# Gate rows of the second block through a scratch row in device memory, and a regrouped opening

## The reference

```python
h = h + 0.5 * rmsnorm(swiglu(rmsnorm(h, g[0]), ffn1_w_in[i], ffn1_w_out[i]), g[1])
...
h = h + rmsnorm(mix, g[3])
h = h + 0.5 * rmsnorm(swiglu(rmsnorm(h, g[4]), ffn2_w_in[i], ffn2_w_out[i]), g[5])
h = h + rmsnorm(sigmoid(h @ ple_w_gate[i]) * (p[i] @ ple_w_proj[i]), g[6])
```

```python
sh1, sc1, g1, sh2, sc2, g2 = jnp.split(s_lat @ ada_w[i] + ada_b[i], 6, axis=-1)
a_l = modulate(rms_norm(h_lat, norm_g[i, 0]), sh1, sc1)
...
h_lat = h_lat + g1 * y_l            # one gate value per column, the same for all tokens
h_lat = h_lat + g2 * sq_relu_mlp(modulate(rms_norm(h_lat, norm_g[i, 1]), sh2, sc2), w1, w2)
```

## Time and profile before

| | |
|---|---|
| median of 3 runs | 1859.18 us (1859.07 to 1860.43) |
| the profiled execution | 1859.91 us, span 1857.8 us |
| PE busy | 1839.6 us, 99% |
| DVE, ACT, POOL busy | 1370.5, 950.6, 127.7 us |
| DMA | 380.68 MB, mean 205 GB/s |

### The profile page before, as it was taken

The page is one execution under the profiler, slowest core; times in us unless marked ns, Lnnn a source line. Parts: engine busy times, 40 slices in busy tenths (PEclk is TensorE's granted clock), DMA queues, the critical chain, the costliest instruction groups (busy, mean ns, idle before and its releaser), DMA issues.

```text
span 1857.8 us, 23263 instructions
## 1 busy us (share of the span) xinstructions
PE 1839.6 (99%) x9008; PEld 1522.6 (82%) x9008; DVE 1370.5 (74%) x1649; ACT 950.6 (51%) x1414; POOL 127.7 (7%) x177
## 2 busy tenths in 40 slices
PE   9999999999999999999999999999999999999998
PEld 6788888888878887887888888888888888888886
DVE  7898866977879777845598987777676558766665
ACT  5444564544464445544465435754564447555443
POOL 0430001000010000000020001100200001000000
PEclk9999999999999999999999999999999999999999
DMA  9787434877568775554496865545555546226552
GB/s 346 270 294 260 165 141 129 288 255 265 201 207 291 238 261 192 183 186 158 140 324 224 292 205 192 177 143 203 184 181 182 192 171 204 92 91 215 182 182 91
DMA packets 197374, 380.68 MB, mean 205 GB/s; under 512 B 13616, under 2 KB 101424, under 8 KB 197264
## 3 DMA queue, kind: packets, MB, share of 16 engines
q1 hardware_dynamic: 194336, 370.88, 58.5%
q0 software_dynamic: 2208, 7.73, 1.2%
q10 hardware_dynamic: 720, 0.58, 0.1%
HBM read 378.11 MB, written 1.05 MB: 204 GB/s over the span
## 4 chain that ended last, share of the span: by engine, by line
PE 93%; DVE 4%; DMA 1%; ACT 1%; issue 1%; POOL 0%; ACTq 0%; DVEq 0%; POOLq 0%; SPq 0%
PE ps L514 16%; PE ps L515 16%; PE ps L519 16%; PE ps L507 8%; PE ps L509 8%; PE ps L508 8%; PE ps L1312 7%; PE ps L531 4%; PE ps L1317 4%; DVE w_lo L2355 1%; DMA raw<-ffn_w_in_dram 1%; PE ps L762 1%; PE ps L1460 1%; PE ps L720 1%; PE ps L1484 1%
## 5 line engine op out<-in xcount | busy, mean ns | idle before, releaser
L2355 DVE TENSOR_TENSOR w_lo<-raw,w_hi 128x1024 fp32r<-128x1024 f32 x600 | 713.0, 1226 | 147.8 <-ACT w_hi L1612 143.4
L1612 ACT ACTIVATE w_hi<-raw 128x1024 fp32r<-128x1024 f32 x599 | 610.6, 1055 | 231.5 <-PE ps L519 139.8
L514 PE MATMUL ps<-w_hi,xt 128*128 128x512 f32 x692 | 275.5, 398 | 0.0
L515 PE MATMUL ps<-w_hi,xt 128*128 128x512 f32 x692 | 269.9, 390 | 0.0
L514 PE MATMUL ps<-w_hi,ht_hi 128*128 128x512 f32 x664 | 261.4, 394 | 0.2 <-DVE ht_lo L2560 0.2
L515 PE MATMUL ps<-w_hi,ht_lo 128*128 128x512 f32 x664 | 258.5, 389 | 0.0
L507 PE MATMUL ps<-w_hi,xt 128*128 128x512 f32 (+1 forms) x588 | 231.2, 393 | 3.9 <-DVE xt L2626 1.9
L509 PE MATMUL ps<-w_hi,xt 128*128 128x512 f32 (+1 forms) x588 | 227.6, 387 | 0.0
L508 PE MATMUL ps<-w_lo,xt 128*128 128x512 f32 (+1 forms) x588 | 227.3, 387 | 0.0
L2539 DVE SCALAR_TENSOR_TENSOR tmp<-arena,s_col,tmp 128x1024 f32<-128x1024 f32 x168 | 210.2, 1292 | 0.0
L519 PE MATMUL ps<-w_lo,xt 128*128 128x512 f32 x692 | 185.0, 389 | 0.0
(11 more groups left out here) (309 smaller groups left out, 2024.8 us busy)
## 6 DMA issues: line engine op xcount, KB each, us to landing
raw<-mlp_w_dram SPq DMA_DIRECT2D x192, 512.0 KB, 4.4
raw<-ffn_w_in_dram SPq DMA_DIRECT2D x168, 512.0 KB, 5.7
arena<-ada_w_dram SPq DMA_DIRECT2D x96, 512.0 KB, 6.2
raw<-ffn_w_out_dram SPq DMA_DIRECT2D x88, 512.0 KB, 4.5
raw<-odd_w_in_dram SPq DMA_DIRECT2D x48, 512.0 KB, 4.7
raw<-attn_w_qkv_dram SPq DMA_DIRECT2D x24, 512.0 KB, 4.9
raw<-even_w_in_dram SPq DMA_DIRECT2D x22, 512.0 KB, 4.6
raw<-ple_w_gate_dram SPq DMA_DIRECT2D x16, 512.0 KB, 3.9
```

Source lines behind the costliest of these rows:

```text
L514: pe.matmul(dst, a_hi, hi, start=start, stop=False)
L515: pe.matmul(dst, a_lo, hi, start=False, stop=False)
L1612: act.activation(w_hi[:, slot, c], raw[:, slot, c], ACT.Copy).then_inc(S(f"hi{slot}"), 1)
L2355: TT(w_lo[:, slot, c], raw[:, slot, c], w_hi[:, slot, c].bitcast(F32), ALU.subtract).then_inc(S(f"lo{slot}"), 1)
```

## The change

Gate rows: `gate_row`, `gate_copy` and the waits for them go. After each layer's conditioning vectors are done, ACT writes the gate columns to a tensor `gate_rows` in device memory, with one DMA for each gate (`gates_out(0)` four, `gates_out(1)` two, each of 128 x 8 single elements of 4 bytes), and later reads each row back with a DMA that broadcasts 4 KB to 128 partitions (`gate_in`, seven). `gates_out(0)` stands on ACT where the first half-row copy stood in `ffn(3)`.

```diff
+            def gates_out(l):
+                act.wait_ge(S("mod_set"), l + 1)
+                for j, part in enumerate((2, 5)):
+                    for v in range(2 - l):
+                        act.dma_start(T["gate_rows"][l, j, v].rearrange("(k p) -> p k", p=P), ada_of(l, part, v),
+                                      allow_slow_non_contiguous=True).then_inc(S("gates_out"), 16)
+
+            def gate_in(dst, signal, l, part, v):
+                act.wait_ge(S("gates_out"), (64, 96)[l])
+                act.dma_start(dst[:], T["gate_rows"][l, part // 3, v].partition_broadcast(P)).then_inc(S(signal), 16)
...
                 if run == 3:
-                    act.wait_ge(S("mod_set"), 1)
-                    gate_copy(table, 0, 6)
+                    gates_out(0)
                 split((1,) if run == 0 else (0, 1))
...
+                    if run == 3 and i == 3:
+                        gate_in(table, "gate_c", 0, 2, 1)
...
-                if i == 0:
-                    gate_row(0, 5, 0, (0, 1), 6)
-                elif i == 1:
-                    gate_row(1, 2, 0, (0, 1), 6)
-                elif i == 7:
+                if i == 7:
                     wait_xn()
                     xn_fill(0, xn_c)
...
                     act.wait_ge(S("p_free"), 8)
-                    gate_copy(gain, 0, 6)
-                    gate_copy(gain, 1, 7)
+                    gate_in(gain, "gate_l", 0, 5, 0)
+                    gates_out(1)
```

Opening: the host lays input and first weights side by side (`first_t`, 3 KB per partition and k) and SP alone loads them, one DMA per k (k = 3 in two). ACT issues only `norm_t`. The highs and lows are made as before, from `first_w` in `arena`. PE begins a k with its two products of highs and waits for each low only ahead of the products that read it:

```diff
+                    pe.wait_ge(S("x_hi"), 2 * k + 2)
+                    for m in range(MT):
+                        pe.matmul(bank(m), xt_hi[:, k, m * P:(m + 1) * P], hi, start=k == 0, stop=False)
                     if k in (0, 2):
                         pe.wait_ge(S("lo_first"), k // 2 + 1)
-                    elif k != 5:
+                    else:
                         slab(slot, uses, k // 2 % 2)
+                    for m in range(MT):
+                        pe.matmul(bank(m), xt_hi[:, k, m * P:(m + 1) * P], lo, start=False, stop=False)
                     pe.wait_ge(S("x_lo"), 2 * k + 2)
                     for m in range(MT):
-                        last = products(k, m)
+                        last = pe.matmul(bank(m), xt_lo[:, k, m * P:(m + 1) * P], hi, start=False, stop=False)
```

Small rows: `attn_sinks` and `hgrn_onorm_g` are laid in one array `mix_rows` by the host and loaded with one broadcast of 136 floats:

```diff
-                        first_rows()
+                        sp.dma_start(small[:, 120:256], T["mix_rows"].partition_broadcast(P)).then_inc(S("rows_in"), 16)
```

More of the change, by code:

```diff
@@ L282, in build @@
         rd = small[:, 80:96]
[L283 removed]
+        sink_b = small[:, 120:128]
         onorm_b = small[:, 128:256]
@@ L404, in ffn @@
                     sp.dma_start(vec_t[:], T["vec_cols"]).then_inc(S("vec_in"), 16)
-                    load(wide(wo, 0))
+                    slot, uses = ring.take()
+                    sp.wait_ge(S(f"hi{slot}"), 2)
+                    for src, view in wide(wo, 0):
+                        sp.dma_start(view(slot), src).then_inc(S(f"raw{slot}"), 16)
                     ada_load(run, 0)
@@ L736, in wait_xn @@
                 pe.wait_ge(S("xn_dve"), n["xn"])
[L738 to L745, removed]
             def pool_turn(src, g, b):
@@ L1756, in ffn @@
                 k = (n["sq"] - 1) % 4 if run else 0
-                split((0, 1), "raw2_half" if run == 0 else None)
+                split()
                 def swish(j, k_back, b0=4):
@@ L1849, in _ @@
             for half in range(2):
[L1850 to L1856, removed]
+                act.wait_ge(S(f"raw{s1}" if half else "raw1_half"), 32)
+                k = 4 + 2 * half
+                act.activation(cut(w_hi[:, s1, 1024 * half:1024 * half + 1024], 2, 512), first_w[:, k:k + 2],
+                               ACT.Copy).then_inc(S(f"hi{s1}"), 1)
+                first_high(k)
+                first_high(k + 1)
             n["x"] += 1
@@ L2585, in ffn @@
                     split()
-                    ada_sums(third)
-                    gated(base + i + 1)
+                    if run == 0 and i == 1:
+                        gated(base + i + 1)
+                        ada_sums(third)
+                    else:
+                        ada_sums(third)
+                        gated(base + i + 1)
                     if run == 0 and i == 5:
-                        dve.wait_ge(S("rows_in"), 64)
+                        dve.wait_ge(S("rows_in"), 32)
                         TT(lb_diff, lb_in[:, 0], lb_in[:, 1], ALU.subtract).then_inc(S("e_lb_in"), 1)
@@ L2634, in _ @@
                 c = slice(512 * k, 512 * k + 512)
-                TT(w_lo[:, s0, c], raw[:, s0, c], w_hi[:, s0, c].bitcast(F32),
+                TT(w_lo[:, s0, c], first_w[:, k], w_hi[:, s0, c].bitcast(F32),
                    ALU.subtract).then_inc(S(f"lo{s0}") if k % 2 else S("lo_first"), 1)
@@ L2638, in _ @@
             for half in range(2):
-                split_half(s1, u1, half)
-                first_low(4 + 2 * half)
-                first_low(5 + 2 * half)
+                dve.wait_ge(S(f"hi{s1}"), half + 1)
+                k, c = 4 + 2 * half, slice(1024 * half, 1024 * half + 1024)
+                TT(cut(w_lo[:, s1, c], 2, 512), first_w[:, k:k + 2], cut(w_hi[:, s1, c].bitcast(F32), 2, 512),
+                   ALU.subtract).then_inc(S(f"lo{s1}"), 1)
+                first_low(k)
+                first_low(k + 1)
             n["x"] += 1
@@ L2960, in gated_sums, with gated_add @@
                     TT(h[:, m, c], h[:, m, c], cut(tmp[:], 2, MT, 512)[:, half, m], ALU.add).then_inc(S(upd), 1)
-            def gated_add(m, h, gate, gates, upd, k_back):
-                dve.wait_ge(S("gate_set"), gates)
+            def gated_add(m, h, gate, landed, count, upd, k_back):
+                dve.wait_ge(S(landed), count)
                 if m == 0:
```

154 lines of the change are left out of this document (65 added, 89 removed).

## The result

The changed kernel takes 1876.16 us (median of five runs, 1866.11 to 1880.68) against 1859.18 before (1859.07 to 1860.43): ratio 1.0081, 95% interval 1.007 to 1.0091. It is slower, clear of the interval, and outside the forecast range. The runs of the kernel before lie within 1.4 us of each other, these within 15. The profiled execution is the fastest of the five: 1866.11 us, span 1864.0. So the trace shows 6 of the 17 us of the median; the other executions of this kernel have no trace.

A forecast was written before the change was run, and what follows sets the result against it. PE, busy 99% of the span, was taken to bound the kernel: 1859.9 - 4.4 (turns) - 1.5 (opening) - 0.9 (sinks) + 1.0 (writes) = 1854.1, as a median 1853.4 us. Range 1851.5 to 1860, likeliest case 1851.8 to 1855.4.

The forecast's parts named there:

- The opening: Start of kernel: x_t and first weights in order on SP bring the next stage to 18.0 us, saving 1.5 us.
- The sinks: Near 66 to 90 us: sinks and onorm as one broadcast end SP's hold and PE's wait, saving 0.9 us.
- The turns: Gate turns on PE: 48 fewer at two sites of four and five of eight, saving 4.4 us.
- the last site: Last site of eight turns: saves nothing, since PE sits idle 1.58 us behind it until DVE has xt ready.
- The broadcasts: Seven gate-row reads on ACT, 512 KB each: cost 0, covered by PE's products; uncovered, 4.2 us at a reader.
- The writes: Element writes ahead of the splits near 946 us: ACT held 2.8 us, PE stalled about 1.0 us.
- the positions end: Rate bound from the positions load, some 500 packets per us: 2 us for a write of 1024 elements.
- 2T - 3.4: Stall near 946 us in terms of T, the time of one 1024-element write; gains gone at T = 5.1.
- Rival 1: Slow element writes hold ACT, 946 to 965 us: stall 12 us at the sinks rate, total 1864.4; chance 0.13.
- Rival 2: The writes starve SP's weights as well: 31 us without weights, 22 us lost, total 1874; chance 0.05.
- The slack: Splits near 946 us: without a hold, a slip of 1.2 against a slack of 3.4 costs 0.

The follow-up runs named there:

- opening: Kernel before with only the change's opening and small rows, gates still by turns and copies: 1857.55 us, ratio 0.9989.
- blocks_late: Kernel of 512-byte gate pieces (blocks) with the four write issues moved from ahead of run 3's splits to the end of step 1: 1854.34 us, ratio 0.9971.
- spread: Changed kernel with the four writes of gates_out(0) issued on ACT one per step, in steps 0 to 3 of ffn(3): 1863.77 us, ratio 1.0019.
- pool: Changed kernel with the same element writes issued from POOL instead of ACT: 1868.43 us, ratio 1.0045.
- pair: The run writes with two of its four element writes ahead of run 3's splits: 1872.07 us, ratio 1.0067.
- none: The run writes without its four element writes ahead of run 3's splits, the two later ones kept: 1857.54 us, ratio 0.999.
- blocks: Changed kernel with each gate turned once on PE, copied once per layer and written as eight pieces of 512 bytes: 1855.66 us, ratio 0.9977.
- writes: The run opening, turns and copies kept, plus the six element writes into a scratch row nobody reads: 1873.36 us, ratio 1.0076.
- spaced: The run writes with each 4-byte element placed 512 bytes from the next: 1864.5 us, ratio 1.0027.
- gates: Kernel before with the gate part of the change alone, on the old opening: 1871.31 us, ratio 1.006.
- run 7: Not a run's label: in "its fastest run 7" the 7 is the loss in us of the changed kernel's fastest run, 1866.11 us.

## Why the prediction was wrong

- **The opening: right, and by the forecast road.** Forecast 1.5 us and 18.0 for the first product of the next stage; 18.04 measured. Between 5 and 6 us the DMA engines move 379 GB/s instead of 278. The last lows on DVE are done at 15.08 instead of 16.16, and the last twelve products begin right behind them (timelines of DVE and PE):

```profile
14.20 0.88 DVE L2605 SCALAR_TENSOR_TENSOR xt<-arena,norm_t,xt 128x256 fp32r<-128x256 f32 x2
```

```profile
15.22 0.47 PE L505 MATMUL ps<-w_hi,xt 128*128 128x512 f32 x1 [0.28 <-DVE xt L2605]
```

- **The sinks: right.** Forecast 0.9; their broadcast lands in 6.1 us, and PE doesn't wait near 90. Both together were to give 2.4: at 943.00 the kernel is 2.54 ahead, and opening as a whole gained 2.1.
- **The turns: right but for the last site.** Seven sites stood there, six of which were to give 4.4 us and the last nothing. Its 0.87 us have indeed become wait: 1.58 ahead of the product before, 2.45 now (timeline of PE).

```profile
1675.89 0.77 PE L505 MATMUL ps<-w_hi,xt 128*128 128x512 f32 x1 [2.45 <-DVE xt L2487]
```

  But the longer wait took the clock down in this execution, so the site did not give 0: it cost 1.1 us. Blocks_late, which has six turns where opening has 48, is 3.2 us under opening in its median. The six cost about 0.7 by the spacings of the earlier trace rows (0.44 for four), so 4.4 less 0.7 makes 3.7 expected; the two groups of its runs give about 4.1 and 2.5.
- **The broadcasts: right.** They cost nothing that a wait shows: blocks_late has the same ones. They are six, not seven, so ACT has 12 issues for 13 in the forecast; nothing hangs on that.
- **The writes: the step that failed.** "I take the positions end, since the gate rows' sources and destinations are all distinct, and keep the other." It took the passing of packets for the time of a write. 256 elements read from device memory in half a microsecond said nothing of elements written into it: in spread the packets of a write pass at more than that rate, and yet the weights crawl for eight microseconds after them. Forecast: 2 us for a write of 1024 elements, a hold of 2.8 and a stall of 1.0. Measured: 12.7 to 19.8 us to landing; issues three and four take 3.85 and 5.81 us, 8.9 more than two like the first; a wait of 6.6 us and two more. And the stall expected, 1.0 us, isn't what the prediction's own formula 2T - 3.4 gives at T = 2, which is 0.6. The other end of the bound, 7.7 us, lay too low too.
- **What rivals 1 and 2 said.** Rival 1's place was right: the third and fourth issues, ahead of the same splits. But its formula, 2T - 3.4, would give 22 to 36 us with these landings; the queue takes a new DMA well before the old one has landed. Rival 2 was the larger: with the hold gone (pool, pair) the weights still starve and some 14 us go (pool against blocks_late, pair against none). It priced that at 1874, two under the median; that this comes so near is luck. Its 22 us came from four writes of 7.7 us, one after the other, without any weights; in the trace the four overlap and PE's waits are 9.9 us. What was held against it, "sinks and weights shared one queue, these do not", is wrong: SP's weights fall to 1 to 45 GB/s under writes from ACT's queue and from POOL's. The Trainium skill, DMA: Bandwidth & Descriptors, Queues, rings and completion order, says that the queues share the same DMA engines; by that rule the writes were to be felt on SP's queue, and the runs agree, but how much and for how long it doesn't say. The rule on strided last dimensions (the Trainium skill, the same page, Rules for kernel authors), which the prediction set beside its 1.0 us, spoke rightly against the change.
- **The same page of the Trainium skill**, under Specifications, gives 512 bytes as the smallest transfer for full rate, and says that below it the DMA does a read-modify-write. That the 512 byte pieces of blocks hold nothing up fits with it. It doesn't tell writes from spaced, whose pieces are 4 bytes too and yet land in half the time. No run shows the read-modify-write itself.
- **The slack.** "A slip of 1.2 against a slack of 3.4" looked only at PE's first use of the split. Blocks slipped by 1.5 and lost 1.0 near 960: DVE, which makes w_lo behind the same splits, had less in hand than PE.
- **Left out:** the clock. After its 6.6 us wait PE ran for 3.1 us at 1.2 GHz, in pair for 5.1: 1.6 to 2.6 us on top of a wait.

**What stays open.** Gates alone loses 11.6 us and the opening gains 2.1, so the whole should lose 9.5; its median loses 17, its fastest run 7. Why executions of one kernel differ by 15 us isn't shown; the spread comes with the gates (7 us in gates, 10 in spread, 1 in opening). There is a lead: the second place of writes costs PE no wait in the profiled execution of the changed kernel, its fastest, but 2.1 us in that of none and 5.0 in that of spread, their longest, each with the clock at 0.50 behind it. Whether that makes the longer executions of the changed kernel can't be told, since they have no trace. Nor is it shown why two writes hold up the weights almost as long as four, and whether it is the device memory or the DMA engines that work slowly then; in the window of spread the engines are busy for a share of 0.43 only.

## What to carry to other kernels

A DMA of single elements into device memory costs what it does to everybody else's transfers, not its own 4 KB. So price it with a row of a write, and where there is none, give that end of the range its weight. When a layout change can be had from TensorE in one turn, write rows of 512 bytes or more. An issue belongs behind the splits or copies that feed the busiest engine, and the slack to check is that of every consumer down the chain, not only the first.

## What the runs showed of the hardware

- Four writes of 128 x 8 elements of 4 bytes, side by side: 12.7 to 19.8 us to landing, 13.7 to 18.7 in writes; two alone 17.1 and 21.3; 512 bytes apart 6.3 to 9.5. The same data in 512 byte rows has no landing in the trace; its packets have all passed 5.4 us after the first issue (944.6 to 950, blocks).
- Such writes bring the traffic of all queues, weights above all, down to 1 to 45 GB/s instead of some 280, starting some time after the first issue (changed kernel: 304 GB/s until 949, 105 to 122 until 956, then 1) and lasting until about the moment at which the last one has landed (968.7 and 971 in the changed kernel, 965.5 and 967 in pair). One single write gives eight microseconds of it, in spread after its packets have passed.
- With two such DMAs outstanding ACT's third issue takes 3.9 to 4.2 us and the fourth 2.6 to 5.8 (changed kernel, writes, spaced), where the first two take 0.4 and 0.7 to 1.0.
- The granted clock is at 0.50 from 952.2 on, in an idle stretch of PE that began at 949.3, and stays there until 959, while PE works again from 955.9 on. A wait of PE of 2.45 us was followed by 3.4 us at 0.50 in the changed kernel (1675.8) and in blocks (1667.2); a like wait at the same place was not in blocks_late, gates, spread and pool.
